# Moving the additions of the fifth modulation vector to other units of the output projection

## What is computed

```python
    m_l = (silu_c @ ada_w[i] + ada_b[i]).reshape(bsz, 1, N_MOD, D_MODEL)
    n_l = modulate(rmsnorm(h_lat, norm_g[i, 0]), m_l[:, :, 0], m_l[:, :, 1])
    y_l = chunk_mlp_mix(n_l, a_w_in[j], a_g_v[j], a_w_s[j], a_b_s[j], a_w_out[j])   # (u * s) @ w_out
    h_lat = h_lat + m_l[:, :, 2] * y_l
    n_l = modulate(rmsnorm(h_lat, norm_g[i, 1]), m_l[:, :, 3], m_l[:, :, 4])
    h_lat = h_lat + m_l[:, :, 5] * conv_ffn(n_l, ...)
```

## Time and profile before

| | us |
|---|---|
| median of 3 runs | 2316.59 |
| lowest and highest run | 2311.09, 2317.96 |
| the profiled execution | 2314.23 |
| its span, first to last instruction | 2312.5 |
| PE busy in the span | 2272.0 (98%) |
| DVE busy | 1568.4 (68%) |
| ACT busy | 1133.6 (49%) |
| POOL busy | 104.7 (5%) |
| output projection in the span | about 447 to 629.5 |

### The profile page before, as it was taken

One profiled execution on the slowest core, in us unless ns is written; L12 is line 12 of the kernel. 1 busy time (PEld: TensorE's weight loads), 2 busy tenths in 40 slices (PEclk: granted clock), 3 DMA queues, 4 the chain that ended last, 5 costly groups with the idle time before them and its releaser, 6 DMA issues.

```text
span 2312.5 us, 34533 instructions
## 1 busy us (share of the span) xinstructions
PE 2272.0 (98%) x13302; PEld 1986.6 (86%) x13302; DVE 1568.4 (68%) x2106; ACT 1133.6 (49%) x1696; POOL 104.7 (5%) x203
## 2 busy tenths in 40 slices
PE   6999999999999999999999999999999999999998
PEld 5788888888888888888888889999999999878987
DVE  6888777777788865666656767566566645655655
ACT  3355444434455543555445554444544444555544
POOL 0010100111100000000000001000000000100000
PEclk9999999999999999999999999999999999999999
DMA  9999788799867765555655565444444545544453
GB/s 368 387 385 395 250 276 268 250 325 317 292 218 252 248 200 191 182 184 184 196 182 199 186 198 167 150 155 139 142 148 144 164 149 162 168 135 124 138 184 126
DMA packets 230042, 493.06 MB, mean 213 GB/s; under 512 B 9682, under 2 KB 12520, under 8 KB 226824
## 3 DMA queue, kind: packets, MB, share of 16 engines
q1 hardware_dynamic: 210384, 432.05, 55.1%
q0 software_dynamic: 14272, 50.99, 6.7%
q10 hardware_dynamic: 5256, 8.20, 1.0%
HBM read 488.49 MB, written 2.10 MB: 212 GB/s over the span
## 4 chain that ended last, share of the span: by engine, by line
PE 89%; DMA 5%; DVE 3%; issue 1%; SPq 1%; ACT 0%; POOL 0%; POOLq 0%; DVEq 0%
PE ps L1863 34%; PE ps L1910 22%; PE ps L1925 14%; PE ps L1927 7%; PE ps L2380 4%; DMA mods<-in_ada_w 2%; DMA ada<-in_ada_w 2%; PE ps L2203 1%; SPq L415 1%; DVE acc L1189 1%; PE ps L2365 1%; PE ps L2222 1%; PE ps L2021 1%; PE ps L2349 1%; DVE acc L1132 0%
## 5 line engine op out<-in xcount | busy, mean ns | idle before, releaser
L1123 DVE TENSOR_TENSOR wlo<-raw,whi 128x1024 fp32r<-128x1024 f32 x720 | 872.8, 1222 | 507.1 <-ACT whi L584 505.9
L584 ACT ACTIVATE whi<-raw 128x1024 fp32r<-128x1024 f32 x720 | 756.9, 1057 | 828.5 <-PE ps L1863 402.2
L1925 PE MATMUL ps<-xt__59,whi 128*128 128x512 f32 x1408 | 498.3, 399 | 1.5 <-DVE h L1339 0.7
L1927 PE MATMUL ps<-xt__59,wlo 128*128 128x256 f32 x1408 | 395.4, 281 | 0.0
L1863 PE MATMUL ps<-whi,xt__59 128*128 128x512 f32 x1024 | 330.0, 399 | 6.9 <-DVE xt__59 L1258 6.9
L1925 PEld LDWEIGHTS ps<-xt__59,whi 128*128 128x128 f32 x1408 | 264.5, 188 | 68.8 <-DVE h L1339 2.2
L1910 PE MATMUL ps<-xmh__60,whi 128*128 128x272 f32 x1088 | 322.7, 297 | 0.6 <-DVE h L1339 0.3
L1910 PE MATMUL ps<-xmh__60,wlo 128*128 128x272 f32 x1088 | 314.9, 289 | 0.0
L1910 PE MATMUL ps<-xml__61,whi 128*128 128x272 f32 x1088 | 313.0, 288 | 0.0
L1927 PEld LDWEIGHTS ps<-xt__59,wlo 128*128 128x128 f32 x1408 | 266.0, 189 | 0.1
L1863 PEld LDWEIGHTS ps<-whi,xt__59 128*128 128x128 f32 x1024 | 195.9, 191 | 48.7 <-issue 7.8
(11 more groups left out here) (336 smaller groups left out, 3246.0 us busy)
## 6 DMA issues: line engine op xcount, KB each, us to landing
raw<-in_a_w_in SPq DMA_DIRECT2D x128, 1024.0 KB, 5.3
raw<-in_ffn_w_up SPq DMA_DIRECT2D x88, 1024.0 KB, 5.1
ada<-in_ada_w POOLq DMA_DIRECT2D x96, 512.0 KB, 4.6
raw<-in_a_w_out SPq DMA_DIRECT2D x48, 1024.0 KB, 5.9
raw<-in_ffn_w_down SPq DMA_DIRECT2D x44, 1024.0 KB, 5.1
mods<-in_ada_w SPq DMA_DIRECT2D x64, 512.0 KB, 11.0
raw<-in_b_w_in SPq DMA_DIRECT2D x32, 1024.0 KB, 5.4
ada<-in_ada_w SPq DMA_DIRECT2D x16, 1024.0 KB, 10.9
```

What stands on the lines that cost most here:

```text
L584: act.activation(whi[:, r % 4], raw[:, r // 2, r % 2], ACT.Copy).then_inc(hi_ready, 1)
L1123: dve.tensor_tensor(wlo[:, r % 4], raw[:, r // 2, r % 2], whi[:, r % 4].bitcast(F32), ALU.subtract).then_inc(lo_ready, 1)
L1925: pe.matmul(both, whi[:, r % 4, i, c * P:c * P + P], xt_[:, :, k * T:k * T + T], start=first and i == 0, stop=last and i == 1, skip_group_ ...
L1927: mm = pe.matmul(ps[:, bank + c, 0:T], wlo[:, r % 4, i, c * P:c * P + P], xth[:, k, :], start=False, stop=last and i == 1, skip_group_chec ...
```

## The change

Only the table `ADA4_AT` changes. The list has 32 places before and after. Block 0 keeps its seven. In block 1 the run of t = 8 to 14 becomes pairs with a unit between them, and t = 1 and 15 are new; block 2 has places at 0, 1, 5, 6, 7, 9, 10, 12, 13, 15; block 3 has 1 in addition to 0, 4, 5 and 6. The code below the table stands one line higher, so line 1123 is 1122 in the changed kernel, 1132 is 1131, and so on.

```diff
--- before.py
+++ after.py
@@ -155,9 +155,8 @@
 
 
 
-ADA4_AT = [(0, t) for t in (6, 8, 9, 10, 11, 13, 14)] + [(1, t) for t in (0, 4, 5, 6, 8, 9, 10, 11, 12, 13, 14)]\
-    + [(2, t) for t in (0, 4, 5, 6, 8, 9, 10, 12, 13, 14)]\
-    + [(3, t) for t in (0, 4, 5, 6)]
+ADA4_AT = [(0, t) for t in (6, 8, 9, 10, 11, 13, 14)] + [(1, t) for t in (0, 1, 5, 6, 8, 9, 11, 12, 14, 15)]\
+    + [(2, t) for t in (0, 1, 5, 6, 7, 9, 10, 12, 13, 15)] + [(3, t) for t in (0, 1, 4, 5, 6)]
 ADA5_OUT_AT = (7, 8, 9, 10, 11, 12, 13, 14)
 ADA5_FIRST_AT = (10, 12, 14, 15)
 ADA5_AT = (0, 2, 6, 8, 10, 14)
```

## The result

| | before | changed |
|---|---|---|
| median of 22 runs, us | 2315.89 | 2319.89 |
| lowest and highest | 2307.55, 2319.27 | 2313.18, 2323.51 |
| the profiled execution | 2314.23 | 2322.29 |
| its span | 2312.5 | 2320.6 |

The changed kernel is slower: ratio 1.0019, 95% interval 1.0013 to 1.0026, that is 4 us where I had forecast 1.3 us less. In 12 further runs, beside 35 of before, the ratio was 1.0010 (1.0001 to 1.0019). The size is within the 0.3% that I called no change; the sign is not mine, and the median lies just above the upper end of my range.

What follows compares the result with a forecast made beforehand. TensorE, busy 89% of the span, was taken as the bound, so only its stalls count: 2314.23 - 1.3 = 2312.9 profiled, other parts 0; with the median 2.4 above the profiled run, 2315.3 us, range 2310.5 to 2319.5.

Steps and rivals of the forecast that it cites:

- VectorE's 31.6 us: Output projection: VectorE's 20 waits for half-tile transfers, claimed nearly all swallowed by its lead and not on the path.
- the 0.86: Output projection: busy share of the DMA engines, which the prediction said the weight slabs cause.
- Part 1: Column block 1, unit 15: breaking the run of seven additions removes TensorE's stall, -1.3 us.
- Part 2: Start of block 1: additions of units 0 and 1 ahead of the residual update cost 0 to 0.3 us, taken as 0.
- Part 3: Boundary of blocks 1 and 2: four additions in a row, then a residual; about 3 us lead left, no cost.
- Part 4: Boundary of blocks 2 and 3 and the tail: unit (3,15) fits with 0.2 us to spare; cost 0, at worst +1.3.
- one period of 7.65: Time in us for a pair of additions (addition, load issue, landing), measured in block 1 of the kernel before.
- Both signs: End of projection: (3,15) waiting for its low part, or block 2's residual starting later than 582, would show wrong steps.
- (b): Rival, chance 0.14: a slow load at (3,1) delays the residual, stalling (3,15) +1.2 us, +1.5 in all: 2317.8 to 2318.1.
- (a): Rival, chance 0.27: the tail takes the gain back, (3,15) waits instead of (1,15), time 2316.6 us.
- (d): Rival, chance 0.03: the load is no limit and the order of additions is of no account, 2316.6 us.
- (c): Rival, chance 0.09: unprofiled runs lose more at block 1's run of seven, so the change gives 5 us, 2311.6.

Runs made afterwards that it cites:

- lighter loads: Changed kernel with loads of the fifth and sixth vector cut to 256 KB, results wrong, only time counts: median 2314.57 us against 2316.14, ratio 0.9993.
- Block 1 alone: Kernel before with only block 1's places spread, blocks 2 and 3 unaltered; run twice: medians 2314.14 and 2314.88 us, ratios 0.9994 and 1.0000.
- the short tail under the old table: Kernel before with six instead of eight sixth-vector additions in block 3, two moved to the feed-forward part: median 2315.42 us against 2315.79, ratio 0.9993.
- the second profile: Profile from rerunning the changed kernel with no edit: projection 157.87 us; that rerun's median 2318.42 us against 2315.80, ratio 1.0010.
- block 2 as before: Changed kernel with block 2's places put back to those of the kernel before, blocks 1 and 3 as changed: median 2317.94 us against 2316.14, ratio 1.0003.
- only (3,1): Kernel before with one addition moved, unit 10 of block 1 out, unit 1 of block 3 in: median 2316.75 us, ratio 1.0004.
- without (3,1): Changed kernel with the addition at unit 1 of block 3 moved to unit 4 of block 1: median 2317.08 us, ratio 1.0003.

## Why the prediction was wrong, point by point

**What bounds the kernel: right.** TensorE's waits in the projection price the change, VectorE's 31.6 us do not. The kernel with lighter loads takes 26 us off VectorE's waits of the changed kernel and ends only 1.7 below before. Every profile without a TensorE wait for a low part has 157.54 to 157.56 us. One reading was loose: the 0.86 that I put down to the weight slabs is the share of all transfers in that stretch, the half-tiles included.

**Part 1, the stall at (1,15), -1.3 us: right, with a reservation.** Block 1 alone shows 1.30 and 1.29 in its profiles and -1.1 +- 0.4 in its runs. The reservation is the profile of the short tail under the old table, where the run of seven stands and nothing waits. The stall is a matter of how late the loads land in one execution.

**Part 2, (1,1) ahead of a residual: right.** I had the residual of block 0 starting 0.2 to 4.3 us later; it came 3.2 later after (0,8) (25.26 against 22.09), and (1,3) didn't wait.

**Part 3, the boundary of blocks 1 and 2: no stall, as forecast, but the lead was wrong.** I had the residual of block 1 start when TensorE ends the block, and about 3 us of lead left at (2,3). In the second profile it was 2.9. In the first (1,15) waited 1.9 us for its load and (2,0) and (2,1) 1.4 and 0.9; the residual started 4.3 us after TensorE had ended the block (at 540.35), and the low part of (2,3), the first of the two in the last row, was ready at 548.5, 0.3 us ahead of TensorE:

```profile
544.66 0.69 DVE L1334 TENSOR_TENSOR gy<-ps,acc 128x512 f32<-128x512 f32 x1
...
547.32 2.35 DVE L1122 TENSOR_TENSOR wlo<-raw,whi 128x1024 fp32r<-128x1024 f32 x2
```

And I stopped at (2,3) and never walked the places 5, 6 and 7 behind it, three in a row right after a residual. In the changed kernel the addition of (2,7) waits 3.51 us for its load, and (2,12) comes 96.4 after (0,8), where block 1 alone has it at 94.1 and 94.8. With this delay the walk enters the next boundary. The front of block 2 is not its only source: with block 2 as before (2,12) came at 96.1, and the residual of block 2 was as late.

**Part 4, the step that failed.** I set (2,15) at 571.6, bound by its own cast, and (3,1) one period of 7.65 later. In the span of before these are 100.9 and 108.5 after (0,8). Measured: 104.7 and 112.1 in the first profile, 101.0 and 110.1 in the second. In the first it is the start of the run that was set 3.8 us too early, since the delay that VectorE brings along from further back was put at nothing; the period behind it was 7.3. In the second the start was right to 0.1 us and the period was 9.1 instead of the 7.65 that I took from block 1. The residual, forecast 110.9 after (0,8), came at 114.40 and 112.42. Both signs that the prediction had named for a wrong step were there, the wait at (3,15) and the late residual, and VectorE's waits for half-tiles rose to 37.5 us where they were to fall below 31.6. The spare time at (3,15) was 0.2 us by my own working, and I priced a step with so thin a cover at nothing; measured, 2.41 and 0.19 us of waiting at (3,15), and 3.9 at four units in the first profile. A cover thinner than the scatter of the landings that feed it (4.24 to 8.34 in the rows I had) is no cover.

**The rivals.** (b) named the mechanism, the place (3,1) and the stall at (3,15), and was given 0.14 and +1.5 us. Its price was too low: it took the load of (3,1) alone as slow. That fits the second profile, where this load landed in 7.07 us. In the first it landed in 5.35, but the four ahead of it, for (2,12), (2,13), (2,15) and (3,0), took 6.20, 6.87, 6.34 and 6.49, and 3.9 us of waits at four units came of it. (a), the tail takes the gain back, is the same mechanism at its mild end, and the second profile looks like it. Together they held 0.41 to the forecast's 0.47; they should have been one case, and the likelier one. (d) is refuted by the lighter loads. What (c) said, that unprofiled runs lose more at (1,15), has nothing for it.

**The range.** Its top was set from rival (b) and the scatter of the runs as if the two did not add. 2319.89 lies 0.4 us above it.

**What the parts cost**, from the means: block 1 spread -1.1; (3,1) +2.3 (only (3,1) against block 1 alone, first run), +2.7 (block 2 as before against block 1 alone) or +3.0 (changed, +3.6, against without (3,1)); block 2's table +1.7 (without (3,1) against block 1 alone) or +2.0 (changed against block 2 as before). -1.1 + 2.7 + 1.8 = 3.4, against 3.6 measured over 34 runs. Each of these has an error of 0.7 or more.

**What stays open.** Why loads land later in some executions than in others wasn't found, nor how often each kernel has the long wait. In the two profiles of the changed kernel the projection and what follows it cost 3.7 us more and 0.45 less than before, 1.6 on average, where the means of all runs differ by 3.6; what makes up the rest no profile shows. The shift of 4 us ahead of (0,8) is a second scatter on top of it, and one profile of a kernel can't tell how often it comes.

## What to carry to other kernels

Work on a helper engine that stands in a run must be priced by the lead it hands on: walk the engine from one point where it waits for the bounding engine to the next such point, through everything between, and not place by place. Moving work from a place where it costs a little to one just ahead of an incompressible run (here a residual and eleven paced additions) can cost more than it gave. If the spare time at the end of such a walk is smaller than the scatter of the transfers in it, forecast the stall, not its absence.

## What the runs showed of the hardware

A load of 512 KB landed in 5.8 us in the median while slabs of 1 MB were in flight beside it, one of 256 KB in 3.4. The rule that I had weighed against the rows, from the Trainium skill ("DMA: Bandwidth & Descriptors", anatomy of one DMA from GpSimd), gives 3.2 and 2.6 us as estimates: the measured difference between the sizes is 2.4 us, four times the 0.6 between the estimates. Here the measurement decides; that the sharing with the slabs makes the difference to the estimates is my reading and was not tried apart.

After the wait of 4.05 us at (3,15), with nothing on TensorE, the granted clock fell; after the wait of 2.25 us in the changed kernel it did not. The stretches of the kernel with block 2 as before, ahead of the wait, over it, and behind it (PEclk is the third number from the end):

```profile
620.00:629.00 9.00, 9.00 (x41) 7.26 (x39) 4.97 (x5) 3.19 (x3) 1.05 (x2) 1.00 0.91 314
629.00:634.00 5.00, 0.95 (x4) 0.66 (x4) 4.96 (x5) 1.06 (x1) 0.53 (x1) 1.00 0.45 147
634.00:638.50 4.50, 4.50 (x18) 3.61 (x17) 3.38 (x6) 0.61 (x1) 0.00 (x0) 0.62 0.91 304
```

From 634.40 the matmuls start 0.43 us apart, the pace of the lower level of 1.2 GHz, against 0.23 at 2.4. Some eight matmuls at 0.2 us more each add 1.6 us to the wait: this stall cost more than its length, the one of 2.25 us did not. Between the two nothing was measured.
